# Loads of bias rows, steps of modulation and the order of two mixers' side work in a two-block transformer kernel

## The chip, the cores and the metric

One core of one Trainium2 chip runs the whole program. Its engines are TensorE (PE, with its weight loads as PEld), VectorE (DVE), ScalarE (ACT), GpSimd (POOL, unused here) and SyncE (SP), which issues nearly all DMA transfers from one in-order queue. The metric is the device time of one execution in microseconds (us), the median of several.

## The reference

The input is x of 256 tokens by 1024. The first block adds a hybrid mixer (dilated attention and a state space scan) and a SwiGLU; the second adds two layers. Each of those is modulated by a condition vector, and the second of them has the mixer that most of the change is about. Cut to what matters:

```python
mx = jnp.split((c_act @ w_mod[l] + b_mod[l])[:, None, :], N_MOD, axis=-1)   # modulation, 2 layers
x = x + 0.5 * mx[2] * swiglu_2(modulate(rms_norm(x), mx[0], mx[1]), *ffn1)
h = modulate(rms_norm(x), mx[3], mx[4])
# layer 0: mix_window_diff (heads of h @ ab_w_in); layer 1, the last mixer:
cq, dq, ckv, dk, dv = split_cols(h @ w_in, CD_SPLITS)              # 768, 512, 288, 512, 512
ckv_c, dk_c, dv_c = split_cols(hc @ w_in[:, CD_Q_WIDTH:], CD_SPLITS[2:])
q = mla_queries(cq, c_q_a_norm, c_w_uq, ...)                       # low rank norm, then up
kn, kr, v = mla_keys_values(ckv, c_kv_a_norm, c_w_ukv, ...)
y_mla = sweep_blocks(lambda q_blk, n: mla_attend(q_blk, kn_all, kr_all, v_all), q, Q_BLOCK)
y_nat = neighbourhood_attention(dq, dk, dv, dk_c, dv_c, d_rpb)     # with a relative bias per grid offset
y = jnp.concatenate([y_mla, y_nat], axis=-1) @ w_out
x = x + mx[5] * y
x = x + 0.5 * mx[8] * swiglu_2(modulate(rms_norm(x), mx[6], mx[7]), *ffn2)
```

## The kernel before, in words

Every matrix is cut into chunks of 128 by up to 1024 numbers (up to 512 KB). A chunk goes through a ring of six slots: SP loads it (`load_chunk`, L283) once the chunk six places before it has been used, ACT rounds it to a high part (`split_hi`, L289), DVE takes the low part (`split_lo`, L295), and PE multiplies high by high, high by low and low by high (`product`, L347). ACT and DVE split three chunks ahead of PE (`LEAD`). Results lie in three PSUM banks; a bank is free again when ACT has copied it out (L422 for `LinearT`) or DVE has (L442, L449).

The program is a list of stages, each with steps. A step has a part for SP, PE, ACT and DVE, and every engine runs its parts in the order of one common list. So a wait in one step holds all that stands behind it on that engine, and SP's transfers of later steps are issued only after those of earlier steps. `woven` mixes tracks of stages by their share of the segment; `beside(base, side, per)` (L1315) puts side steps after the base step that their number names, at most `per` of them after each.

Three places matter here.

**Modulation** (L668). Per layer, 9 rounds of 8 chunks of `w_mod` (512 KB each) are multiplied with the two condition vectors: 8 matmuls of the profile a chunk, on four 32 column tiles of the array (`chunk`, L725). They have a ring of six slots of their own. A step is two chunks; a further step of each round turns the row of results (L712). Layer 0's stage is woven along the first block's projections, layer 1's from 0.1 to 0.95 of the segment that ends the first block, and that begins with the last chunks of `w_attn_branch`, the eight of `w_out`, and the norm before the feed-forward. SP loads six chunks at the stage's first step, and then the chunk that is six places on whenever one is used.

**Head work.** `HeadNorms` normalises the heads of a projection (squares on ACT L1358, sums on DVE L1371, the scale L1362 and L1363 on ACT, the products L1381 to L1398 on DVE; item j is applied in step j + 2). `Turns` transposes them on PE (L1450) through one bank, which ACT empties (L1460) before the next turn may begin. Both are side steps, of projections and of attention.

**The last mixer.** Its 44 weight chunks are those of cq (6), ckr for x and for the context (4 and 4), dk (4 and 4), dq (4), dv (4 and 4), w_uq (6) and w_ukv (2 and 2). `GridLoad` is one stage ahead of them: when all of the modulated norm is there, SP issues 32 transfers of 64 KB each, in pieces of 64 numbers, that lay out the bias rows of neighbourhood attention (`grid_rows`). Then `Attend` works on pairs of heads, 8 pairs of the neighbourhood and 8 of the low rank attention: scores L1519 (and the bias by L1525), maxima on DVE (L1604 or L1615), exponentials on ACT (L1561), transposes L1536, values L1548, each pair spread over four steps. `mla_heads` (the norms of the low rank queries and keys, steps `m_steps`), `SpreadKeys` and the turns of their results stand beside these pairs.

```python
        alone(norm, grid_load, Merged(beside(steps_of(*cd_main[1:], u_q, u_kv_x, u_kv_c), side, per=2)))
        side = [(0, (spread, 0)), (0, m_steps[4]), (0, m_steps[5])]
        side += [(1, m_steps[6]), (1, m_steps[7]), (1, t_steps[14]), (1, t_steps[15])]
        side += [(2, m_steps[8]), (2, m_steps[9]), (2, t_steps[16]), (2, t_steps[17])]
        side += [(3 + n // 2, t_steps[18 + n]) for n in range(8)]
```

## Time and profile before

| | us |
|---|---|
| median of 3 runs (2728.10 to 2730.65) | 2728.46 |
| the profiled execution | 2728.05 |
| its span in the trace | 2726.2 |
| PE busy (15262 matmuls) | 2538.7, 93% of the span |
| PE weight loads busy | 2152.0, 79% |
| DVE busy | 1350.0, 50% |
| ACT busy | 1018.4, 37% |
| moved by DMA | 372.23 MB, 137 GB/s in the mean |

The span is the time from the first to the last instruction of the trace; 1.85 us of the execution lie around it. The chain of waits, followed back from the end, is 85% PE. The granted clock has two levels, 2.4 GHz (1.00 in the rows) and 1.2 GHz (0.50); its mean is 0.965. So the time is that of PE's work and of the places at which PE stands still or goes slowly, and these are what is looked for.

### The profile page before, as it was taken

How to read it: one execution, taken by the hardware profiler on the slowest of the kernel's cores; microseconds unless marked ns; L12 is line 12 of the kernel's file. 1: busy time of each engine (PE TensorE's matmuls, PEld its weight loads, DVE VectorE, ACT ScalarE, POOL GpSimd, SP SyncE). 2: the span in 40 equal slices, each digit the busy share in tenths (PEclk: the TensorE clock that was granted, in tenths of full speed). 3: DMA queues.
4: the chain of work that ended last, by engine and by line, in shares of the span. 5: the costliest groups of instructions: out<-in, count | busy, mean ns of one | idle time of the engine just before them, and what ended most of it. 6: DMA issues, size and time to landing. Idle time of an engine off the chain costs nothing.

```text
span 2726.2 us, 36254 instructions
## 1 busy us (share of the span) xinstructions
PE 2538.7 (93%) x15262; PEld 2152.0 (79%) x15262; DVE 1350.0 (50%) x2221; ACT 1018.4 (37%) x1633; POOL 0.2 (0%) x4
## 2 busy tenths in 40 slices
PE   7999999899989999989778999998999986978998
PEld 6888789888867888868566888886888866758998
DVE  4646464654454333357866333334333344656654
ACT  4534444433343222145542222223222224643542
POOL 0000000000000000000000000000000000000000
PEclk8999999999989999989889999999999997989999
DMA  8886743488843333335002333332333325502554
GB/s 280 281 270 194 227 128 101 156 312 305 312 143 93 93 101 93 101 109 185 16 1 77 94 100 93 101 93 77 96 98 98 95 76 146 166 7 63 164 185 132
DMA packets 145476, 372.23 MB, mean 137 GB/s; under 512 B 20234, under 2 KB 65570, under 8 KB 145186
## 3 DMA queue, kind: packets, MB, share of 16 engines
q1 hardware_dynamic: 144882, 368.21, 42.9%
q8 instruction: 122, 2.00, 0.3%
q10 hardware_dynamic: 432, 1.69, 0.2%
q14 instruction: 40, 0.33, 0.0%
HBM read 368.71 MB, written 1.15 MB: 136 GB/s over the span
## 4 chain that ended last, share of the span: by engine, by line
PE 85%; DVE 7%; ACT 4%; issue 1%; SPq 1%; DMA 1%; ACTq 0%; DVEq 0%
PE psum L347 74%; PE psum L725 2%; PE psum L1548 1%; PE psum L1519 1%; DVE normed_raw L533 1%; DVE normed_lo L546 1%; PE psum L1536 1%; SPq L1798 1%; PE psum L1450 1%; PE psum L1138 1%; PE psum L939 1%; ACT weights_hi L289 1%; PE psum L494 1%; PE psum L1150 1%; ACT arena L1561 1%
## 5 line engine op out<-in xcount | busy, mean ns | idle before, releaser
L295 DVE TENSOR_TENSOR weights_lo<-weights_raw,weights_hi 128x1024 fp32r<-128x1024 f32 (+3 forms) x547 | 657.6, 1213 | 528.5 <-ACT weights_hi L289 525.9
L347 PE MATMUL psum<-normed_hi,weights_hi 128*128 128x256 f32 (+1 forms) x2560 | 864.4, 338 | 34.7 <-DVE normed_lo L546 23.8
L347 PE MATMUL psum<-normed_lo,weights_hi 128*128 128x256 f32 (+1 forms) x2560 | 848.5, 331 | 0.0
L347 PE MATMUL psum<-normed_hi,weights_lo 128*128 128x256 f32 (+1 forms) x2560 | 847.6, 331 | 0.0
L289 ACT CAST weights_hi<-weights_raw 128x1024 fp32r<-128x1024 f32 (+3 forms) x547 | 563.0, 1035 | 394.8 <-DMA weights_raw<-in_w_down 266.9
L347 PEld LDWEIGHTS psum<-normed_hi,weights_hi 128*128 128x128 f32 x2560 | 489.4, 191 | 119.9 <-issue 53.1
L347 PEld LDWEIGHTS psum<-normed_hi,weights_lo 128*128 128x128 f32 x2560 | 490.3, 192 | 44.8
L347 PEld LDWEIGHTS psum<-normed_lo,weights_hi 128*128 128x128 f32 x2560 | 490.7, 192 | 43.9 <-issue 1.2
L347 PE MATMUL psum<-hidden_hi,weights_hi 128*128 128x512 f32 x528 | 205.4, 389 | 0.0
L347 PE MATMUL psum<-hidden_lo,weights_hi 128*128 128x512 f32 x528 | 205.4, 389 | 0.0
L347 PE MATMUL psum<-hidden_hi,weights_lo 128*128 128x512 f32 x528 | 205.4, 389 | 0.0
L347 PE MATMUL psum<-weights_hi,normed_hi 128*128 128x512 f32 (+3 forms) x368 | 144.5, 393 | 40.3 <-ACT arena L422 20.9
L449 DVE SCALAR_TENSOR_TENSOR resid<-psum,mod,resid 128x256 f32<-128x256 f32 x80 | 35.8, 480 | 275.4 <-PE psum L347 275.4
L585 DVE TENSOR_TENSOR arena<-arena,psum 128x512 f32<-128x512 f32 (+1 forms) x110 | 64.0, 581 | 205.4 <-PE psum L347 205.4
L577 ACT CAST hidden_hi<-arena 128x512 fp32r<-128x512 f32 x66 | 41.0, 621 | 309.3 <-DVE arena L585 309.3
L574 ACT ACTIVATE arena<-psum 128x512 f32<-128x512 f32 (+1 forms) x110 | 56.4, 513 | 247.7 <-PE psum L347 247.6
L347 PE MATMUL psum<-weights_hi,normed_lo 128*128 128x512 f32 (+3 forms) x368 | 140.6, 382 | 0.0
L347 PE MATMUL psum<-weights_lo,normed_hi 128*128 128x512 f32 (+3 forms) x368 | 139.8, 380 | 0.0
L347 PEld LDWEIGHTS psum<-weights_hi,normed_hi 128*128 128x128 f32 x368 | 75.6, 205 | 57.1 <-ACT arena L422 21.1
L347 PEld LDWEIGHTS psum<-hidden_hi,weights_lo 128*128 128x128 f32 x528 | 99.1, 188 | 20.7
L347 PEld LDWEIGHTS psum<-hidden_lo,weights_hi 128*128 128x128 f32 x528 | 99.1, 188 | 20.6
L347 PEld LDWEIGHTS psum<-hidden_hi,weights_hi 128*128 128x128 f32 x528 | 99.1, 188 | 20.4
(254 smaller groups left out, 2794.1 us busy)
## 6 DMA issues: line engine op xcount, KB each, us to landing
weights_raw<-in_w_gu SPq DMA_DIRECT2D x220, 512.0 KB, 3.5
weights_raw<-in_w_down SPq DMA_DIRECT2D x110, 512.0 KB, 3.5
arena<-in_w_mod SPq DMA_DIRECT2D x72, 512.0 KB, 6.3
weights_raw<-in_w_x SPq DMA_DIRECT2D x24, 512.0 KB, 4.7
resid<-in_w_mod SPq DMA_DIRECT2D x24, 512.0 KB, 6.1
normed_raw<-in_w_mod SPq DMA_DIRECT2D x24, 512.0 KB, 5.8
under_normed_hi<-in_w_mod SPq DMA_DIRECT2D x24, 512.0 KB, 6.4
weights_raw<-in_w_qk SPq DMA_DIRECT2D x24, 512.0 KB, 4.0
```

Of the source, the lines that this page charges most:

```text
L289: se.copy(w_hi[:, c % RING, a], w_raw[:, c % RING, a]).then_inc(hi_ready, 1)
L295: ve.tensor_tensor(w_lo[:, c % RING, a], w_raw[:, c % RING, a], w_hi[:, c % RING, a].bitcast(F32), ALU.subtract).then_inc(lo_ready, 1)
L347: last = te.matmul(out, a, b, start=start and n == 0, stop=stop and n == 2)
L449: last = ve.scalar_tensor_tensor(out=resid[:, k, mine], in0=psum[:, self.bank(k), side * S - at0:(side + 1) * S - at0], scalar=mod[:, m, s ...
L494: last = te.matmul(psum[:, NORM_BANK, 0:w], ones, self.squares_at[:, k, :], start=(k == 0), stop=(k == KD - 1))
L533: last = ve.scalar_tensor_tensor(out=dest[:, k, a], in0=resid[:, k, a], scalar=self.gain(k, side), in1=rstd[:, a], op0=ALU.mult, op1=ALU.mult)
L546: last = ve.scalar_tensor_tensor(out=lo[:, a], in0=raw[:, a], scalar=self.shift(k - 1, side), in1=hi[:, a].bitcast(F32), op0=ALU.add, op1= ...
L574: se.activation(raw, self.sums(b), ACT.Silu).then_inc(evac_act, 1)
L577: se.copy(hi, raw).then_inc(hid_hi, 1)
L585: ve.tensor_tensor(raw, raw, self.sums(b), ALU.mult).then_inc(evac_dve, 1)
L725: last = te.matmul(psum[32 * g:32 * g + 32, MOD_BANK, 0:MOD_W], cond[:, k, :], self.ring[c % MOD_RING][:, g, :], start=k == 0, stop=k == K ...
L939: last = te.matmul(psum[:, SIDE + i % 2, j * S:(j + 1) * S], ident[0:SH, h:h + 1].to_broadcast([SH, P]), la_t, start=True, stop=True)
```

## The change

Four things are done. Modulation takes four chunks to a step, so that a round has two such steps and one that turns. The grid loads become a stage of eight steps of four transfers, one after every second weight chunk of the last mixer from its first chunk on. In the last mixer dq comes before dk, dv of the context comes last, behind w_uq and w_ukv, and the head work is set anew: the first eight steps of `mla_heads`, `SpreadKeys` and two turns stand beside projections, and attention begins with what is left. In the layer before, the last four head norms and four turns beside attention come three steps later, and two side steps may follow one step.

```diff
@@ class Modulation
-                self.n = MOD_ROUNDS * (KD // 2 + 1) + 1
+                self.n = MOD_ROUNDS * (KD // 4 + 1) + 1
...
-                r, k = divmod(i, KD // 2 + 1)
-                return self.first + r, 2 * k - 2
+                r, k = divmod(i, KD // 4 + 1)
+                return self.first + r, 4 * k - 4
...
-                    for m in range(2):
+                    for m in range(4):
                         self.load(sp, (r - self.first) * KD + k + m + MOD_RING)
...
-                    self.chunk(pe, r, k)
-                    self.chunk(pe, r, k + 1)
+                    for m in range(4):
+                        self.chunk(pe, r, k + m)
@@ class GridLoad
+            n = NT * 4
...
-                sp.wait_ge(*self.after)
-                for t in range(NT):
-                    for rl in range(2):
-                        for h in range(8):
+                if i == 0:
+                    sp.wait_ge(*self.after)
+                t, pair = divmod(i, 4)
+                for rl in range(2):
+                    for h in (2 * pair, 2 * pair + 1):
@@ attention of layer 0
-        side = [(0, s) for s in h_steps[14:18]] + [(4, s) for s in t_steps[10:14]]
+        side = [(3 + n, step) for n, step in enumerate(h_steps[14:18])]
+        side += [(7 + n // 2, step) for n, step in enumerate(t_steps[10:14])]
...
-        alone(Merged(beside(steps_of(attend), side)))
+        alone(Merged(beside(steps_of(attend), side, per=2)))
@@ the last mixer
-                (x_t, "w_ckr", KVR + ROPE, ckr), (ctx_t, "w_ckr", KVR + ROPE, ckr),
-                (x_t, "w_dk", WT, dk), (ctx_t, "w_dk", WT, dk), (x_t, "w_dq", WT, dq),
-                (x_t, "w_dv", WT, dv), (ctx_t, "w_dv", WT, dv))])
+                (x_t, "w_ckr", KVR + ROPE, ckr), (ctx_t, "w_ckr", KVR + ROPE, ckr), (x_t, "w_dq", WT, dq),
+                (x_t, "w_dk", WT, dk), (ctx_t, "w_dk", WT, dk), (x_t, "w_dv", WT, dv))])
...
+        cd_main += [u_q, u_kv_x, u_kv_c, LinearT(W["w_dv"], KD, WT, normed, ctx_t, dv)]
...
-        side += [(28, t_steps[n]) for n in range(8, 12)] + [(30, t_steps[12]), (30, t_steps[13])]
+        side += [(22, h_steps[12]), (22, h_steps[13]), (24, t_steps[8]), (24, t_steps[9])]
+        side += [(26, h_steps[14]), (26, h_steps[15]), (27, h_steps[16]), (27, h_steps[17])]
+        side += [(28 + n, t_steps[10 + n]) for n in range(4)]
         m_steps = steps_of(mla_heads)
-        side += [(40, m_steps[n]) for n in range(4)]
-        alone(norm, grid_load, Merged(beside(steps_of(*cd_main[1:], u_q, u_kv_x, u_kv_c), side, per=2)))
+        side += [(36 + n, m_steps[n]) for n in range(4)] + [(40, m_steps[4]), (40, m_steps[5])]
+        side += [(41, (spread, 0)), (41, m_steps[6]), (42, t_steps[14]), (42, t_steps[15]), (42, m_steps[7])]
+        base_steps = beside(steps_of(*cd_main[1:]), [(2 * n, step) for n, step in enumerate(steps_of(grid_load))])
+        places = [n for n, (stage, _) in enumerate(base_steps) if stage is not grid_load]
+        side = [(places[j], step) for j, step in side]
+        alone(norm, Merged(beside(base_steps, side, per=2)))
         segments[-1] = (segments[-1][0], 0)
-        side = [(0, (spread, 0)), (0, m_steps[4]), (0, m_steps[5])]
-        side += [(1, m_steps[6]), (1, m_steps[7]), (1, t_steps[14]), (1, t_steps[15])]
-        side += [(2, m_steps[8]), (2, m_steps[9]), (2, t_steps[16]), (2, t_steps[17])]
-        side += [(3 + n // 2, t_steps[18 + n]) for n in range(8)]
+        side = [(0, m_steps[8]), (0, m_steps[9]), (0, t_steps[16]), (1, t_steps[17])]
+        side += [(1 + n // 2, t_steps[18 + n]) for n in range(8)]
```

Left out are the renumbering of the head items and turns that follows from dq standing before dk, and the copy of a modulation round, which now waits in the step that begins at chunk 4 of it.

The SP queue at the start of the last mixer (weights_raw<-in_w_... is a weight chunk, arena<-scratch_rpb a grid transfer), as a difference:

```order
 L283 DMA weights_raw<-in_w_cq 128x1024 x6
-L1798 DMA arena<-scratch_rpb 64x4x64 x32
-L283 DMA weights_raw<-in_w_ckr 128x576 x8
-L283 DMA weights_raw<-in_w_dk 128x1024 x8
...
+L283 DMA weights_raw<-in_w_ckr 128x576
+L1800 DMA arena<-scratch_rpb 64x4x64 x4
+L283 DMA weights_raw<-in_w_ckr 128x576 x2
+L1800 DMA arena<-scratch_rpb 64x4x64 x4
+L283 DMA weights_raw<-in_w_ckr 128x576 x2
```

The 32 transfers stood in one piece ahead of the seventh chunk; now the seventh chunk goes first, and four transfers stand between every two chunks.

PE at the end of `w_out` in the first block, before (merged is the input of `w_out`, L725 modulation, L490 the sum of the norm, normed the input of the feed-forward):

```order
L347 MATMUL psum<-merged_hi,weights_lo 128x256
L725 MATMUL psum<-arena,cond 32x256 x8
L347 MATMUL psum<-merged_hi,weights_hi 128x256
...
L725 MATMUL psum<-arena,cond 32x256 x8
L490 MATMUL psum<-squares,const 128x256
L725 MATMUL psum<-arena,cond 32x256 x8
L347 MATMUL psum<-normed_hi,weights_hi 128x256
```

and in the changed kernel:

```order
L347 MATMUL psum<-merged_hi,weights_lo 128x256
L725 MATMUL psum<-arena,cond 32x256 x16
L490 MATMUL psum<-squares,const 128x256
L347 MATMUL psum<-normed_hi,weights_hi 128x256
```

Before, the first step of modulation cut `w_out` two chunks from its end, a second stood before the sum of the norm and a third behind it. Now one step of four chunks stands after the last chunk of `w_out`.

PE at the start of attention in the last mixer, before (L1519 and L1525 are a pair's scores, L1450 x8 two turns, L1536 and L1548 transposes and values):

```order
L1519 MATMUL psum<-arena 128x512 x2
L1525 MATMUL psum<-arena,const 128x256 x2
L1519 MATMUL psum<-arena 128x512 x2
L1525 MATMUL psum<-arena,const 128x256 x2
L1450 MATMUL psum<-const,arena 96x128 x8
L1519 MATMUL psum<-arena 128x512 x2
L1525 MATMUL psum<-arena,const 128x256 x2
L1536 MATMUL psum<-const,arena 128x128 x8
L1450 MATMUL psum<-const,arena 96x128 x8
```

and in the changed kernel:

```order
L1519 MATMUL psum<-arena 128x512 x2
L1525 MATMUL psum<-arena,const 128x256 x2
L1450 MATMUL psum<-const,arena 96x128 x4
L1519 MATMUL psum<-arena 128x512 x2
L1525 MATMUL psum<-arena,const 128x256 x2
L1450 MATMUL psum<-const,arena 96x128 x12
L1519 MATMUL psum<-arena 128x512 x2
L1525 MATMUL psum<-arena,const 128x256 x2
L1536 MATMUL psum<-const,arena 128x128 x8
L1450 MATMUL psum<-const,arena 96x128 x8
```

The twelve turns beside attention have become ten: two (L1450 96x128 x8) now stand before the last chunk of dv. The others begin one step sooner and are done at the fifth pair, where before they were done at the seventh.

## Rows read from the trace of the kernel before

**Rows 1.** The waits of PE, whole run (us in total, times, longest us).
```profile
PE psum L347 <- ACT arena L422: 24.2, 4, 20.9
```

**Rows 2.** Timeline of the SP queue (start us, us, what, count).
```profile
2238.22 21.05 SPq L1798 DMA_DIRECT2D arena<-scratch_rpb  x32
```

**Rows 3.** Timeline of ACT in the same stretch (in brackets: idle before, and what ended it).
```profile
2263.71 0.67 ACT L289 CAST weights_hi<-weights_raw 128x576 fp32r<-128x576 f32 x1 [23.60 <-DMA weights_raw<-in_w_ckr]
...
2271.81 0.66 ACT L422 ACTIVATE arena<-psum 128x256 f32<-128x256 f32 x2 [5.31 <-PE psum L347]
```

**Rows 4.** Timeline of TensorE's weight loads in the same stretch.
```profile
2239.53 0.19 PEld L347 LDWEIGHTS psum<-weights_hi,normed_hi 128*128 128x128 f32 x1 [1.39 <-DVE weights_lo L295]
...
2264.93 0.29 PEld L347 LDWEIGHTS psum<-weights_hi,normed_hi 128*128 128x128 f32 x1 [21.14 <-ACT arena L422]
```

**Rows 5.** Busy time in stretches (busy us by engine, clock, DMA share, GB/s).
```profile
50.00:100.00 50.00, 50.00 (x462) 45.12 (x463) 38.97 (x63) 28.05 (x48) 0.00 (x0) 1.00 0.90 287
...
2245.00:2252.00 7.00, 0.00 (x0) 0.00 (x0) 0.00 (x0) 0.00 (x0) 0.00 (x0) 0.59 0.55 101
```

**Rows 6.** Timeline of PE at the start of attention in the last mixer.
```profile
2385.26 1.13 PE L1519 MATMUL psum<-arena 64*128 64x512 f32 x4 [1.17 <-ACT arena L422]
...
2394.29 1.09 PE L1450 MATMUL psum<-const,arena 128*96 128x128 f32 x4 [4.72 <-DVE arena L1398]
...
2401.35 2.08 PE L1519 MATMUL psum<-arena 64*128 64x512 f32 x4
...
2418.12 0.61 PE L1450 MATMUL psum<-const,arena 128*96 128x128 f32 x4 [0.97 <-ACT under_normed_hi L1460]
2418.66 1.13 PE L1519 MATMUL psum<-arena 64*128 64x512 f32 x4
...
2443.97 0.60 PE L1519 MATMUL psum<-under_normed_hi,normed_raw 96*128 96x256 f32 x2
```

**Rows 7.** Timeline of DVE at a maximum there.
```profile
2441.12 0.69 DVE L1615 CUSTOM_DVE_ANT_0 arena<-psum,const 128x512 f32<-128x512 f32 x1 [3.66 <-PE psum L1525]
```

**Rows 8.** Timeline of ACT at an exponential there.
```profile
2442.47 0.72 ACT L1561 ACTIVATE arena<-arena,small 128x512 f32<-128x512 f32 x1 [2.87 <-DVE small L1615]
```

**Rows 9.** The page's costliest groups: count, then busy us and mean ns.
```profile
L295 DVE TENSOR_TENSOR weights_lo<-weights_raw,weights_hi 128x1024 fp32r<-128x1024 f32 (+3 forms) x547 | 657.6, 1213 | 528.5 <-ACT weights_hi L289 525.9
```

**Rows 10.** Timeline of PE around one step of modulation.
```profile
59.73 0.28 PE L347 MATMUL psum<-normed_hi,weights_lo 128*128 128x256 f32 x1
...
60.94 0.39 PE L347 MATMUL psum<-normed_hi,weights_hi 128*128 128x256 f32 x1
```

**Rows 11.** Timeline of PE at the first steps of modulation.
```profile
18.56 0.64 PE L725 MATMUL psum<-resid,cond 128*32 128x256 f32 x8 [2.48 <-DMA resid<-in_w_mod]
...
34.54 1.94 PE L725 MATMUL psum<-normed_raw,cond 128*32 128x256 f32 x16
```

**Rows 12.** Timeline of DVE at the end of w_out in the first block.
```profile
536.37 0.42 DVE L442 TENSOR_TENSOR resid<-resid,psum 128x256 f32<-128x256 f32 x1 [0.28 <-PE psum L347]
...
539.24 0.42 DVE L442 TENSOR_TENSOR resid<-resid,psum 128x256 f32<-128x256 f32 x1 [0.28 <-PE psum L347]
```

**Rows 13.** Timeline of PE in the same place.
```profile
542.46 0.64 PE L725 MATMUL psum<-arena,cond 128*32 128x256 f32 x8 [3.26 <-DMA arena<-in_w_mod]
543.71 1.08 PE L725 MATMUL psum<-arena,cond 128*32 128x256 f32 x8 [0.61 <-DMA arena<-in_w_mod]
...
552.90 1.07 PE L725 MATMUL psum<-arena,cond 128*32 128x256 f32 x16
554.40 0.70 PE L490 MATMUL psum<-squares,const 128*128 128x256 f32 x2 [0.43 <-DVE squares L460]
...
558.02 0.36 PE L347 MATMUL psum<-normed_hi,weights_hi 128*128 128x256 f32 x1 [1.92 <-DVE normed_lo L541]
```

**Rows 14.** Timeline of DVE at the start of attention in the first mixer of the second block.
```profile
1303.10 1.23 DVE L1604 TENSOR_REDUCE small<-psum 128x2 f32<-128x1024 f32 x1 [1.46 <-PE psum L1519]
...
1309.20 0.75 DVE L1627 SCALAR_TENSOR_TENSOR arena<-arena,small 128x512 f32<-128x512 f32 x1
```

More of the change, by code:

```diff
@@ L731, in scalar @@
                 r, k = self.at(i)
-                if k == KD - 2:
+                if k == KD - 4:
                     act.wait_ge(mod_used, KD * (r + 1))
@@ L1991, in build @@
         u_kv_c = LinearT(W["w_ukv"], KVR // P, WT, ckv_t, ctx_t, kv)
+        cd_main += [u_q, u_kv_x, u_kv_c, LinearT(W["w_dv"], KD, WT, normed, ctx_t, dv)]
+        cd_main[-1].ready = norm.ready
         def whole(a, t, start, width):
@@ L2021, in build @@
                                 [part[:, m, :] for part in ckv_t], col("ckv_norm", m), pair=True) for m in range(KVR // P)]
-        turn_items += [TurnItem([dk[:, t, m * P:(m + 1) * P] for t in range(TT)], [heads.done(13)], dk_t[:, m, :])
+        turn_items += [TurnItem([dq[:, t, (m + j) * P:(m + j + 1) * P] for j in range(2) for t in x_t], [heads.done(11)],
+                                dq_t[:, m:m + 2, :], HD ** -0.5) for m in (0, 2)]
+        turn_items += [TurnItem([dk[:, t, m * P:(m + 1) * P] for t in range(TT)], [heads.done(15)], dk_t[:, m, :])
                        for m in range(4)]
-        turn_items += [TurnItem([dq[:, t, (m + j) * P:(m + j + 1) * P] for j in range(2) for t in x_t], [heads.done(15)],
-                                dq_t[:, m:m + 2, :], HD ** -0.5) for m in (0, 2)]
         turn_items += [TurnItem([mq[:, t, (h + j) * MQ:(h + j + 1) * MQ] for j in range(2) for t in x_t], [mla_heads.done(3)],
```

13 lines of the change are left out of this document (6 added, 7 removed).

## The prediction

> **What bounds the kernel now.** I read the waits of PE first, since the chain of waits runs 85% over PE. Most of them are short and spread out; one is not: a single wait of 20.9 us for ACT's copy of a PSUM bank, L422 [rows 1]. The queue of SP shows what is behind it: 32 grid transfers are issued from 2238.22 for 21.05 us, 0.66 us each, and only then the next weight chunk [rows 2]. ACT splits three chunks ahead, so it stands for 23.60 us until that chunk lands, with the copy of the bank behind it in its order [rows 3]; PE starts the chunk at 2239.53, uses what it has, and then waits 21.14 us to load a weight [rows 4]. The stretch inside has a granted clock of 0.59 and DMA engines 55% busy [rows 5], so after the stall PE also goes at the lower of its two levels.
>
> The second place is the start of attention behind it: from the first pair's scores at 2385.26 to the ninth's at 2443.97 take 58.7 us, with waits of PE for turns that wait for head norms [rows 6]. The third is spread over the whole first block: each step of modulation holds PE, and one of them stops it in the middle of `w_out` [rows 10 to 13].
>
> **The grid loads.** 32 issues of 0.66 us stay. They now stand in groups of four, 2.63 us, between pairs of weight chunks. The seventh chunk is issued ahead of them, when chunk 1 is used. The first group waits for the norm as before and is issued from 2238.2 to 2240.9; the eighth and ninth chunk follow at once, before PE needs them. PE starts the fourth chunk at 2239.53 [rows 4]; three chunks at 2.87 us (the distance of two copies [rows 12]) bring it to 2248.1, where the seventh begins. Before, it began when the sixth was copied, 2271.8 [rows 3]. That is **-23.7 us**, slow clock included. The cover of the rest: from here the ckr chunks are small, 0.56 of a full one by their 576 columns, so two of them take PE some 3.2 us, and SP needs 2.63 and two weight issues for them, 3.3 us. SP falls behind by little in three such rounds, and has six slots of lead; then come full chunks, 5.7 us a pair. If that lead were gone, ACT would wait again, some 1 us a round. I add 1 us for it below.
>
> By the Trainium skill, page DMA: Bandwidth & Descriptors, section Issuing engines are not separate DMA queues, the time to initiate a DMA is "usually small relative to the DMA itself". Here the trace differs: the transfers keep the engines 55% busy while SP is busy all the time, so issue is the longer of the two. By the rule the packets would be what holds the weights, and parting the issues would leave most of the stall; that is the first rival.
>
> **Attention of the last mixer.** Before, the first two pairs have 2 head steps and the spreading of keys, then 2 and two turns, then 2 and two turns beside them; the third pair comes 16.1 us after the first and the fifth 33.4 us after it [rows 6]. Now the last two head steps and one turn stand after the first pair, three turns after the second, then two each. I follow it: an operation of DVE over 128x512 is 0.69 us and a maximum is two of them [rows 7], as is the product of one head norm, of which two stand before the second maximum; an exponential is 1.52 [rows 8], a turn 0.6 [rows 6] with as much for its copy. That puts the third pair at 12.7 us after the first, the fourth at 21.4, the fifth at 28.4, the sixth at 35, and the three after it, with no double turn, 4.7 apart: the ninth at 49.5. Before it was 58.7 [rows 6]. **-9 us**. These steps have gone beside the context's dv, four chunks or 11.5 us of PE. DVE has for them four splits of 1.2 us [rows 9] and head work of some 16 operations, 10.9 us, 15.8 in all, so it ends about 1.5 us late for the first maximum, and the first of the two turns waits up to 2. In return the turns of dk stand one to a step: a second turn in a step waits 0.97 us for the first one's copy [rows 6], and three of these go. With the 1 us of SP from above: **+1.5 us**, between -4 (no backlog at all) and +6 (DVE's whole excess over PE's 11.5 us, and the 2 us of the turn).
>
> **Modulation.** A step of two chunks costs PE 1.21 us from the last matmul before to the first after it, less the usual 0.12 (2.87 for 24 [rows 12]): 1.09 [rows 10]. A lone chunk of 8 matmuls takes 0.64, two take 1.07 [rows 13], so a chunk is 0.43 and the change to and from this kind of matmul 0.23; the first matmul after it is longer by 0.11 (0.39 for 0.28 [rows 10]). That makes 0.34 a step. There are 36 steps of chunks a layer, now 18.
>
> Layer 0: 18 fewer steps. One of them was free, since the first stood in PE's wait for the first norm [rows 11]; now the first stands behind the small dt product, where two chunks take 1.94 at the slow clock [rows 11], and I count 1.7 for two more. 17 x 0.34 - 1.7 = **-4.1 us**. PE is busy without a break where I looked (50.00 of 50 us [rows 5]), so this arrives.
>
> Layer 1: the first step waited 3.26 and 0.61 us for its chunks in the middle of `w_out`, and the two last chunks of `w_out` came out at 552.90, partly at the slow clock [rows 13]. Now these run on: 539.24 plus 2 x 2.87 [rows 12] is 545.0. The chunks of modulation landed at 542.46 and 543.71 [rows 13], 1.25 apart, so the fourth at 546.2; the step ends at 546.7. The sum of the norm came 1.5 us behind `w_out`, it is at 547.1 now; from there to the feed-forward 3.6 us as before (554.40 to 558.02 [rows 13]): 550.7 for 558.0, -7.3. By 558.0 six chunks had been done, now four: +0.9. Behind it 33 steps become 17: 16 x 0.34 = 5.4. Together **-11.8 us**. If the fourth chunk lands a burst later, by up to 4 us, that comes off.
>
> By the Trainium skill, page TensorE: Matmul & The Clock Gate, section Part 3: Packing small matmuls, a pack of column tiles takes one matmul's time and some 4 ns a tile; no price for entering or leaving is stated. The trace has 0.34 us a step; by the page the halving of the steps would bring nothing. That is the second rival.
>
> **Attention of layer 0.** The first pair's maximum starts at 1303.10 and its last product at 1309.20 [rows 14]; one head step stands between them, and three more in the next pairs. Without them at most 1309.20 - 1303.10 - 1.2 = 4.9 us can be won, less what comes back: the same four norms later, where DVE also has pairs with a bias, and two steps with two turns, 1 us each by the second turn's wait [rows 6]. Between -4.9 and +2; DVE has slack later, but only part: **-1.5 us**.
>
> **Sum**, against the profiled execution's 2728.05 (0.4 below the median, whose runs lie within 2.6): -23.7 - 9 + 1.5 - 4.1 - 11.8 - 1.5 = -48.6, so 2679.5; I say **2680**. A measurement of this kernel tells 0.2%, 5.5 us, from no change.
>
> **Rivals.**
> - *Packets hold the weights, not issue.* The engines were busy 55% of the 21.05 us [rows 5]: 11.6 us. If this time stays, since every weight chunk lies behind 1024 small pieces, the time is 2680 + 11.6 = 2691.5. For it: pieces of 64 numbers. Against: they are spread over 16 engines and over some 28 us now. Chance 0.12.
> - *A step's price does not halve.* If the 0.34 us belongs to chunks and not to steps, 33 x 0.34 = 11.2 us fall away: 2691. Against: the lone chunk's 0.64 [rows 13]. 0.07.
> - *The backlog of DVE eats the gain of attention.* If head steps beside the context's dv make DVE late by their whole 5 us and the second pair waits for it and the turns too, the 9 us are gone: 2689. 0.12.
> - *More than counted*: layer 0's attention brings its 4.9 and the projections wait less, 2670. 0.04.
> - *Slower: bursts of modulation starve the weights.* In the first block the DMA engines are busy 0.90 at 287 GB/s [rows 5]. A step now asks for four chunks at once, 2.1 MB or 7.3 us at that rate, and a weight chunk asked for behind them lands that much later. Its slack is three chunks of 2.87, 8.6 us, until ACT splits it, and three more until PE. It decides if a step's four loads and the weights between cannot be moved in the time of that step; then PE waits at each of 35 steps. 1.5 us at each undoes the forecast, 2 us gives 2680 + 70 = 2750. Against: the rate needed rises by 2% only (0.34 in 15 us), and the rows show 10% free. 0.03.
>
> **How the numbers follow.** The forecast has 0.62, with its own range 2672 to 2688. The rivals on the slower side of it lie at 2689 to 2692. The range is 2668 to 2693: it takes in all but the last rival and the far ends. Of the last rival's 0.03 a third falls within 0.2%. Faster by over 0.2% 0.97, within 0.01, slower 0.02.
>
> **What would show it.** SP's queue must have eight groups of 2.6 us with weight issues between, and no wait of PE for L422 over 2 us there. The seventh chunk should begin about 2248 less what was gained before (some 17 us), so at 2231. A step of modulation must take 2.07 us from the last matmul before it to the first after it (4 x 0.43 + 0.23 + 0.12). `w_out` must end without a DMA wait inside. The ninth pair must come about 50 us after the first. It is wrong if ACT waits for weights in the last mixer by more than 5 us in all, if DMA waits appear before L725 or L347 in the first block, or if the first pair's scores of the last mixer do not come some 40 us earlier than before.

## The result, and the profile after

The changed kernel takes **2699.49 us** (median of 4, 2697.82 to 2701.74) beside 2728.28 for the kernel before on the same chip: a ratio of 0.9894, interval 0.9877 to 0.9911, or 29 us. The forecast was 2680, the range 2668 to 2693. The direction was right and the size a good half of what was forecast. The profiled execution took 2701.74 us, with a span of 2700.0 (2726.2 before), PE busy 2537.1 us (2538.7) and a mean granted clock of 0.966 (0.965).

**The stall at the grid loads is gone.** The waits of PE of the changed kernel, the line that answers to [rows 1], whose longest was 20.9 us (the 2.8 of it lie in the first block, the rest in the last mixer):

```profile
PE psum L347 <- ACT arena L422: 4.0, 2, 2.8
```

The SP queue of the changed kernel, in place of the one row of 21.05 us in [rows 2]:

```profile
2234.13 0.33 SPq L283 DMA_DIRECT2D weights_raw<-in_w_ckr  x1
2239.94 2.61 SPq L1800 DMA_DIRECT2D arena<-scratch_rpb  x4
2242.60 1.08 SPq L283 DMA_DIRECT2D weights_raw<-in_w_ckr  x2
2243.72 2.56 SPq L1800 DMA_DIRECT2D arena<-scratch_rpb  x4
2246.32 1.18 SPq L283 DMA_DIRECT2D weights_raw<-in_w_ckr  x2
```

These are the first two of eight groups, of 2.6 to 3.2 us, with weights between them; the seventh chunk is issued at 2234.13, ahead of all. PE begins it at 2249.85 (2271.61 before), where the prediction had 2231: the stall is gone, but what was to be gained ahead of it is not there.

**Modulation.** PE around a step of four chunks, which answers to [rows 10]:

```profile
66.29 0.28 PE L347 MATMUL psum<-normed_hi,weights_lo 128*128 128x256 f32 x1
66.50 1.07 PE L725 MATMUL psum<-normed_raw,cond 128*32 128x256 f32 x16
67.39 1.05 PE L725 MATMUL psum<-under_normed_hi,cond 128*32 128x256 f32 x16
68.37 0.39 PE L347 MATMUL psum<-normed_hi,weights_hi 128*128 128x256 f32 x1
```

From 66.29 to 68.37 are 2.08 us; 2.07 was forecast. And the end of `w_out`, as in [rows 13]:

```profile
545.13 1.50 PE L725 MATMUL psum<-arena,cond 128*32 128x256 f32 x24
546.89 0.64 PE L725 MATMUL psum<-arena,cond 128*32 128x256 f32 x8 [0.25 <-DMA arena<-in_w_mod]
547.46 0.70 PE L490 MATMUL psum<-squares,const 128*128 128x256 f32 x2
551.08 0.55 PE L347 MATMUL psum<-normed_hi,weights_hi 128*128 128x256 f32 x1 [2.92 <-DVE normed_lo L541]
```

Forecast were the step at 545.0, the feed-forward at 550.7. It begins at 551.08, where before it began at 558.02.

**The last mixer.** PE at the start of its attention, for [rows 6] (L1519 begins a pair; L1450 is a turn):

```profile
2368.93 1.13 PE L1519 MATMUL psum<-arena 64*128 64x512 f32 x4 [1.17 <-ACT arena L422]
...
2379.22 0.84 PE L1450 MATMUL psum<-const,arena 128*96 128x128 f32 x4 [3.61 <-ACT normed_raw L1460]
2380.84 1.06 PE L1450 MATMUL psum<-const,arena 128*96 128x128 f32 x4 [0.77 <-ACT under_normed_hi L1460]
2381.83 2.08 PE L1519 MATMUL psum<-arena 64*128 64x512 f32 x4
...
2405.48 1.13 PE L1519 MATMUL psum<-arena 64*128 64x512 f32 x4
...
2420.01 0.60 PE L1519 MATMUL psum<-under_normed_hi,normed_raw 96*128 96x256 f32 x2
```

The ninth pair comes 51.1 us after the first (49.5 forecast, 58.7 before), the third after 12.9 (12.7), the sixth after 36.6 (35). But the first pair itself is only 16.3 us earlier than before, where the forecast said some 40. The loss must lie ahead of it.

**Where it lies.** I took the same matmul of PE in both timelines at the borders of the terms. The changed kernel is ahead by 1.1 us at 387, 12.2 at 824, 11.1 at the first pair of attention of layer 0 (1301.93 before). Behind that attention (1442.76 before) it is **1.6 us late**. It is 1.9 late at 2215 and 21.3 ahead at 2269, behind the old stall; 16.3 at the first pair of the last mixer, 24.0 at the ninth. The last 2.3 us of the span's 26.2 come after PE's last matmul. So a term forecast at -1.5 came out at +12.7. Here is PE in that attention, in the pairs beside which the head norms and turns stand now:

```profile
1305.36 1.13 PE L1519 MATMUL psum<-arena 64*128 64x512 f32 x4
1309.30 0.63 PE L1536 MATMUL psum<-const,arena 128*128 128x128 f32 x4 [2.82 <-DVE arena L1627]
...
1310.75 1.13 PE L1519 MATMUL psum<-arena 64*128 64x512 f32 x4
1314.62 1.94 PE L1536 MATMUL psum<-const,arena 128*128 128x128 f32 x8 [2.74 <-ACT arena L1561]
...
1323.89 0.63 PE L1450 MATMUL psum<-const,arena 128*128 128x128 f32 x4 [1.47 <-ACT arena L1460]
1324.45 1.83 PE L1519 MATMUL psum<-arena 64*128 64x512 f32 x4
```

PE stands 2.8 us for DVE (and for the exponential behind it) in one pair after another, then the eight matmuls of L1536 take 1.94 us and the four of L1519 1.83, where they take 1.1 and 1.13 elsewhere, and a second turn in the same step waits 1.47 us for the first one's copy. Such waits stand in the kernel before too, though (3.02 us at 1310.01, 2.13 at 1315.27), so they can't be read as the loss. What the loss consists of shows in the busy time of the whole stretch, from the first pair to the same matmul behind the attention (us of the stretch, then busy us of PE, PEld, DVE, ACT and POOL, the granted clock, DMA share, GB/s). Before, in the changed kernel, and in two kernels of the experiments below, e1 and e6:

```profile
1301.93:1442.76 140.83, 111.92 (x677) 82.76 (x677) 103.22 (x306) 69.22 (x197) 0.00 (x0) 0.89 0.03 8
1290.87:1444.38 153.51, 123.46 (x677) 91.88 (x677) 103.49 (x306) 69.93 (x197) 0.00 (x0) 0.83 0.02 8
1291.76:1433.58 141.82, 113.60 (x677) 83.37 (x678) 103.23 (x306) 69.20 (x197) 0.00 (x0) 0.88 0.03 8
1290.72:1437.42 146.70, 114.03 (x677) 84.07 (x677) 103.38 (x306) 69.58 (x197) 0.00 (x0) 0.88 0.03 8
```

The same 677 matmuls take 11.5 us longer in the changed kernel, at a granted clock of 0.83 for 0.89. The time in which PE does nothing grows by 1.1 us only, from 28.9 to 30.1. So nearly the whole loss is matmuls at the lower clock, and not waiting.

### The profile page after: what moved, and what is told of

Same layout as the page of the kernel before. It is cut to its first block, busy times and chain, and to the rows that moved or that the text cites. A ratio compares the mean times of both kernels' runs of the same rounds, so it can differ in the third digit from the quotient of the medians.

```text
span 2700.0 us, 36253 instructions
## 1 busy us (share of the span) xinstructions
PE 2537.1 (94%) x15262; PEld 2163.9 (80%) x15262; DVE 1350.3 (50%) x2221; ACT 1021.5 (38%) x1633; POOL 0.2 (0%) x4
## 4 chain that ended last, share of the span: by engine, by line
PE 87%; DVE 7%; ACT 4%; issue 1%; DMA 1%; SPq 0%; ACTq 0%; DVEq 0%
PE psum L347 74%; PE psum L725 2%; PE psum L1548 2%; PE psum L1519 1%; DVE normed_raw L533 1%; PE psum L1536 1%; DVE normed_lo L546 1%; PE psum L1450 1%; DVE weights_lo L295 1%; PE psum L1138 1%; PE psum L939 1%; ACT arena L1561 1%; PE psum L1150 1%; DVE arena L1615 1%; ACT weights_hi L289 1%
## 5 line engine op out<-in xcount | busy, mean ns | idle before, releaser
L347 PE MATMUL psum<-normed_hi,weights_hi 128*128 128x256 f32 (+1 forms) x2560 | 863.2, 337 | 36.8 <-DVE normed_lo L546 24.8
L347 PE MATMUL psum<-normed_lo,weights_hi 128*128 128x256 f32 (+1 forms) x2560 | 849.2, 332 | 0.0
L347 PE MATMUL psum<-normed_hi,weights_lo 128*128 128x256 f32 (+1 forms) x2560 | 848.9, 332 | 0.0
L347 PEld LDWEIGHTS psum<-normed_hi,weights_hi 128*128 128x128 f32 x2560 | 490.8, 192 | 112.2 <-issue 47.2
L347 PEld LDWEIGHTS psum<-normed_lo,weights_hi 128*128 128x128 f32 x2560 | 492.1, 192 | 44.0 <-issue 1.2
L347 PEld LDWEIGHTS psum<-normed_hi,weights_lo 128*128 128x128 f32 x2560 | 491.6, 192 | 44.3
L347 PE MATMUL psum<-hidden_hi,weights_hi 128*128 128x512 f32 x528 | 205.4, 389 | 0.0
L347 PE MATMUL psum<-hidden_lo,weights_hi 128*128 128x512 f32 x528 | 205.4, 389 | 0.0
L347 PE MATMUL psum<-hidden_hi,weights_lo 128*128 128x512 f32 x528 | 205.4, 389 | 0.0
L449 DVE SCALAR_TENSOR_TENSOR resid<-psum,mod,resid 128x256 f32<-128x256 f32 x80 | 35.8, 480 | 273.6 <-PE psum L347 273.6
L347 PE MATMUL psum<-weights_hi,normed_hi 128*128 128x512 f32 (+3 forms) x368 | 144.5, 393 | 26.5 <-DVE weights_lo L295 15.3
L347 PE MATMUL psum<-weights_hi,normed_lo 128*128 128x512 f32 (+3 forms) x368 | 139.2, 378 | 0.0
L347 PE MATMUL psum<-weights_lo,normed_hi 128*128 128x512 f32 (+3 forms) x368 | 138.8, 377 | 0.0
L347 PEld LDWEIGHTS psum<-hidden_hi,weights_lo 128*128 128x128 f32 x528 | 99.1, 188 | 20.6
L347 PEld LDWEIGHTS psum<-hidden_hi,weights_hi 128*128 128x128 f32 x528 | 99.1, 188 | 20.6
L347 PEld LDWEIGHTS psum<-hidden_lo,weights_hi 128*128 128x128 f32 x528 | 99.1, 188 | 20.5
L347 PEld LDWEIGHTS psum<-weights_hi,normed_hi 128*128 128x128 f32 x368 | 74.8, 203 | 42.6 <-issue 21.2
```

Source lines behind the costliest of these rows:

```text
L347: last = te.matmul(out, a, b, start=start and n == 0, stop=stop and n == 2)
L449: last = ve.scalar_tensor_tensor(out=resid[:, k, mine], in0=psum[:, self.bank(k), side * S - at0:(side + 1) * S - at0], scalar=mod[:, m, s ...
```

## The experiments

All times are medians, the ratios against the kernel before on the same chip. Every kernel computes the whole reference. The table is the sum of the prediction as measured: what each profiled kernel gains (-) or loses (+) against the profiled kernel before in each stretch, from the starts of the same matmuls of PE (e11 stands apart, below).

| us | median | mod. layer 0, 24 to 387 | mod. layer 1, to 824 | attention layer 0, 1302 to 1443 | grid, 2215 to 2269 | to 1st pair, 2385 | to 9th pair, 2444 |
|---|---|---|---|---|---|---|---|
| forecast | 2680 | -4.1 | -11.8 | -1.5 | -23.7 | +1.5 | -9 |
| the change | 2699.5 | -1.3 | -11.1 | +12.7 | -23.2 | +5.0 | -7.6 |
| e1 | 2689.3 | -1.1 | -11.1 | +1.0 | -23.1 | +4.8 | -9.5 |
| e2 | 2736.0 | -0.3 | -2.0 | +11.4 | -0.8 | -0.8 | -0.1 |
| e3 | 2719.2 | -3.9 | -11.1 | +6.1 | +0.6 | -1.5 | +1.2 |
| e4 | 2708.4 | -0.5 | -2.0 | +7.2 | -22.8 | +2.2 | 0.0 |
| e5 | 2701.8 | -3.7 | -10.8 | +12.2 | -22.6 | +5.5 | -7.5 |
| e6 | 2693.8 | -3.7 | -10.6 | +5.9 | -23.2 | +6.6 | -9.6 |
| e7 | 2726.0 | +0.1 | -1.9 | +4.6 | -0.5 | +4.4 | -9.6 |
| e8 | 2692.9 | -1.1 | -11.2 | +2.6 | -23.2 | +5.1 | -7.7 |
| e9 | 2687.9 | -1.1 | -11.1 | +1.0 | -23.0 | +2.6 | -9.4 |
| e10 | 2693.5 | -3.7 | -10.7 | +1.0 | -23.0 | +5.0 | -9.6 |
| e12 | 2686.2 | -1.3 | -11.3 | +1.1 | -23.0 | +2.4 | -10.7 |

**e1_old_attention0**: the changed kernel with one part undone.

```diff
-        side = [(3 + n, step) for n, step in enumerate(h_steps[14:18])]
-        side += [(7 + n // 2, step) for n, step in enumerate(t_steps[10:14])]
+        side = [(0, s) for s in h_steps[14:18]] + [(4, s) for s in t_steps[10:14]]
...
-        alone(Merged(beside(steps_of(attend), side, per=2)))
+        alone(Merged(beside(steps_of(attend), side)))
```

> The changed kernel with the side steps beside attention of layer 0 as they were before (head norms after steps 0 to 3, turns from step 4 on, one side step after each). Theory A: the new places of these steps cost what the two traces differ by across this attention, from 11.1 us ahead before it to 2.6 us behind after it, 13.7 us. Then this kernel takes 2699.5 - 13.7 = 2686 us (2683 to 2689), and PE is 9 to 12 us ahead of the kernel before at the end of that attention. Rival B: the loss comes with the earlier start of this attention (another phase of TensorE's granted clock), whatever stands beside it. Then this kernel takes 2697 to 2702 us.

2689.26 us (2689.03 to 2690.39), ratio 0.9856 (0.9839 to 0.9872). The attention is back at +1.0. Theory A holds, 0.3 us above its range: 10.2 us in the medians, 11.7 in the traces, and the executions of the two kernels don't meet (2689.0 to 2690.4 and 2697.8 to 2701.7). Of the 11.7 us, 9.9 are PE's busy time (123.46 for 113.60).

**e2_only_attention0**: the same two places, changed on the kernel before.

> The kernel before with the new places of the side steps beside attention of layer 0 and nothing else. Theory A: 2728.3 + 13.7 = 2742 us (2739 to 2745), with waits of PE for DVE at pairs 4 to 6, the lower clock behind them and turns in pairs that PE waits for. Rival B (the loss belongs to the start of attention being earlier): 2726 to 2731 us.

2735.95 us, ratio 1.0024 (1.0013 to 1.0035). Slower, so B falls, but by 7 us and not by 14, although its trace shows +11.4 in the attention. What is wrong is the yardstick: the next two kernels keep the old order there and lose 6 to 7 us against the profiled kernel before all the same. In them PE is busy 119.4 and 123.4 us in this stretch, at a clock of 0.84 and 0.80, where the profiled kernel before has 111.9 at 0.89.

**e3_only_modulation**: the kernel before with the part `class Modulation` of the change.

> The kernel before with only modulation at four chunks to a step. Theory A: by the two traces the changed kernel is 12.2 us ahead once modulation is done, and none of the rest depends on it: 2728.3 - 12.2 = 2716 us (2714 to 2719). Rival B: the earlier start of what follows moves the clock's phase in attention and takes it back: 2726 to 2731 us. In layer 0 I expect the same give-back as in the changed kernel: about 5.5 us ahead at 315 us, 1 to 2 us ahead at 400 us.

2719.21 us, ratio 0.9965 (0.995 to 0.9981): 9.6 us for the 12.2 of A, just above its range. Layer 0 gives 3.9 here and keeps it, against what I expected.

**e4_only_grid_spread**: the kernel before with the grid in eight steps.

```diff
-        alone(norm, grid_load, Merged(beside(steps_of(*cd_main[1:], u_q, u_kv_x, u_kv_c), side, per=2)))
+        base_steps = beside(steps_of(*cd_main[1:], u_q, u_kv_x, u_kv_c),
+                            [(2 * n, step) for n, step in enumerate(steps_of(grid_load))])
+        places = [n for n, (stage, _) in enumerate(base_steps) if stage is not grid_load]
+        side = [(places[j], step) for j, step in side]
+        alone(norm, Merged(beside(base_steps, side, per=2)))
```

> The kernel before with the grid transfers in eight steps of four, one after every second weight chunk of the last mixer, and the old order of its projections and side steps. Theory C: the stall goes (22.9 us in the changed kernel up to the ckr chunks) and nothing of it is given back: 2728.3 - 23 = 2705 us (2703 to 2708), with 58 to 59 us from the first to the ninth pair of its attention. Rival D: the 4.6 us that the changed kernel lost in the projections behind that point come from SP's queue, where the spread transfers stand, not from the new order; then this kernel loses them too and takes 2710 us (2708 to 2713).

2708.39 us, ratio 0.9922 (0.9904 to 0.9941). The time is on the border of C and D; the trace has 22.8 gained and 2.2 given back before the first pair. With the new order alone (e7) 4.4 are given back, with both (e1) 4.8. So most of the 5.0 us belongs to the order, and D holds for at most the smaller half.

**e5_turns_single** and **e6_heads_early** take the change in attention of layer 0 apart (each a diff on the changed kernel):

```diff
# e5
-        side += [(7 + n // 2, step) for n, step in enumerate(t_steps[10:14])]
+        side += [(7 + n, step) for n, step in enumerate(t_steps[10:14])]
-        alone(Merged(beside(steps_of(attend), side, per=2)))
+        alone(Merged(beside(steps_of(attend), side)))
# e6
-        side = [(3 + n, step) for n, step in enumerate(h_steps[14:18])]
+        side = [(n, step) for n, step in enumerate(h_steps[14:18])]
```

> The changed kernel, but beside attention of layer 0 only one side step may follow a step, so that the four turns stand one to a step (7 to 10) and not in two pairs (7 and 8). The head norms keep their new places (3 to 6). The stretch from the first to the thirteenth pair is 53.6 us in the changed kernel and 47.6 before; the pairs with the head norms take 5.4 and 7.3 us there (4.5 and 3.3 before) and the two with paired turns 7.3 and 3.8 behind a 6.4. If the turns in pairs are what costs, this kernel gains 4 us or more: 2693 to 2696 us. If the head norms in the pairs with a bias are (PE stands 2.8 us for DVE in each, and the lower clock follows), it stays at 2698 to 2701 us.

> The changed kernel with the last four head norms of layer 0 beside steps 0 to 3 as before, and the four turns at their new, paired places (steps 7 and 8). If the head norms cost: back to e1_old_attention0 but for two second turns of 1 us, 2689.3 + 2 = 2691 us (2689 to 2693). If the turns cost: 2696 to 2700 us.

e5: 2701.79 us (0.9896, 0.9881 to 0.991), 1 us above the second expectation. e6: 2693.79 us (0.9863, 0.9847 to 0.988), 1 us above the range of what was expected. Moving the head norms back gains 5.7 us. The turns at their new places cost as well: e6 stays 4.5 us above e1 (2 by the ratios, 4.9 in the traces), where 2 were expected. The two costs are of different kinds. In e6 PE's busy time is that of e1 (114.0 for 113.6 us), and it stands still 32.7 us for 28.2: the turns cost waiting. From e6 to the changed kernel the busy time grows by 9.4 us and the standing still falls by 2.6: the later head norms cost clock. The us from one pair to the next (starts of L1519):

```
pair to pair   1-2  ...                                       12-13
change         1.8 3.0 2.8 3.7 3.2 5.4 7.3 6.4 7.3 3.8 4.9 4.0   13-20: 4.9 2.8 6.7 3.8 3.7 3.4 4.1   23-28: 4.6 3.8 3.8 3.8 4.2
e1             1.8 3.0 5.2 6.9 4.5 3.2 3.9 4.3 3.8 3.8 5.2 2.9   13-20: 4.9 2.8 5.1 3.8 3.7 3.4 4.1   23-28: 3.7 2.1 2.5 2.1 4.6
e5             1.8 3.0 2.6 3.9 3.0 5.4 7.2 4.4 4.3 4.3 3.8 2.5   13-20: 3.4 7.3 4.0 5.2 7.0 6.4 5.9   23-28: 4.1 3.2 2.1 2.2 4.9
e4             0.9 3.0 5.2 6.9 4.3 3.5 3.6 4.3 3.8 3.8 5.3 2.9   13-20: 4.9 2.8 5.6 4.9 3.6 3.4 4.1   23-28: 3.9 3.8 3.8 3.8 4.2
```

From the first to the thirteenth pair e5 takes 2.6 us less than e1 (46.2 for 48.8). From the fourteenth to the twentieth it takes 12.9 more (35.8 for 22.9), though no head norm or turn of the moved ones stands there. But e5 does more than part the turns: with one side step to a step, the two steps that normalise the first output tile (L1728, L1742) and its turns, which stand at steps 8, 9, 10 and 12 in e1, are pushed to steps 11 to 14. DVE begins the first of them at 1338.80, ahead of the fourteenth pair's maximum, and in that pair PE waits 3.19 us for DVE. From the fourteenth to the seventeenth pair e5 loses 4.8 us (16.5 for 11.7), and from there to the twentieth 8.0 (19.3 for 11.2), at the lower clock. So e5 doesn't say what paired turns alone cost. Busy time in stretches of e5 (PE, PEld, DVE, ACT, POOL, then clock, DMA share, GB/s):

```profile
1336.00:1344.00 8.00, 4.13 (x25) 2.26 (x23) 6.63 (x23) 4.44 (x12) 0.00 (x0) 1.00 0.00 0
...
1360.00:1368.00 8.00, 8.00 (x38) 7.23 (x37) 4.93 (x16) 2.88 (x9) 0.00 (x0) 0.50 0.01 2
1368.00:1376.00 8.00, 8.00 (x37) 6.90 (x38) 3.38 (x11) 1.61 (x7) 0.00 (x0) 0.50 0.00 0
```

the same of the changed kernel, at pairs 22 to 27:

```profile
1376.00:1384.00 8.00, 4.16 (x29) 3.07 (x28) 6.44 (x30) 5.23 (x19) 0.00 (x0) 0.92 0.00 0
1384.00:1392.00 8.00, 8.00 (x36) 6.36 (x35) 3.85 (x14) 2.97 (x13) 0.00 (x0) 0.50 0.01 2
1392.00:1400.00 8.00, 8.00 (x36) 6.46 (x36) 6.66 (x24) 3.43 (x15) 0.00 (x0) 0.50 0.00 0
```

and of e1, at the pairs of the one (16 to 20) and of the other (24 to 27):

```profile
1352.00:1360.00 8.00, 7.71 (x63) 6.39 (x61) 5.18 (x14) 4.60 (x15) 0.00 (x0) 1.00 0.01 2
1360.00:1368.00 8.00, 7.31 (x61) 6.29 (x60) 6.63 (x24) 3.13 (x12) 0.00 (x0) 1.00 0.01 2
...
1376.00:1384.00 8.00, 5.80 (x45) 4.54 (x45) 5.79 (x26) 5.68 (x21) 0.00 (x0) 1.00 0.01 2
```

At the full clock PE has room in these pairs, little in the one (busy 7.31 to 7.71 of 8 us) and more in the other (5.80). At the lower level it has none, busy 8.00 of 8.00, and a pair of 2.1 to 3.8 us takes 3.8 to 7.0. So the clock decides what the attention costs, and each stretch of 16 us at the lower level is worth 5 us or more. In the changed kernel 5.8 of the 12.7 us are lost up to the thirteenth pair and 5.3 from the 22nd to the 28th, beside which nothing was moved; e4, with the old places, has the same slow stretch there.

**e7_only_last_mixer_order**: the change's last part on the kernel before, with `alone(norm, grid_load, Merged(beside(steps_of(*cd_main[1:]), side, per=2)))`.

> The kernel before with only the new order of the last mixer's projections, head norms and turns; the grid transfers stand in one piece as before. By e1_old_attention0 against e4_only_grid_spread the order brings 27.7 - 20.8 = 6.9 us across the last mixer: 9.5 in the attention, less some 3 that PE waits for DVE beside the last chunks of dv. If it does so without the spread as well: 2729 - 7 = 2722 us (2719 to 2725). If its gain needs the spread (or hides in the clock): within 3 us of before.

2725.99 us, ratio 0.9988 (0.9979 to 0.9997): 3 to 4 us, below the 7 expected and between the two expectations. In the trace 4.4 us are lost ahead of the first pair and 9.6 won up to the ninth, net 5.2. The order works without the spread, for less.

**e8_heads_alternate**, an attempt at something better, on the changed kernel. Left out of the diff are the turns of each tile's output, two steps later (`8 * t + 12` and `8 * t + 14`), and the sorting of the side steps:

```diff
-        side = [(3 + n, step) for n, step in enumerate(h_steps[14:18])]
-        side += [(7 + n // 2, step) for n, step in enumerate(t_steps[10:14])]
+        side = [(2 * n + 1, step) for n, step in enumerate(h_steps[14:18])]
+        side += [(8 + n, step) for n, step in enumerate(t_steps[10:14])]
...
```

> The changed kernel with the four head norms of layer 0 beside steps 1, 3, 5 and 7, the turns one to a step at 8 to 11, and the turns of each tile's output two steps later. If only DVE's total work bounds the first 13 pairs, its place doesn't matter so long as no pair is left waiting behind two head norms in a row: 2686 to 2691 us, as e1_old_attention0 or a little below. If any head norm beside a pair with a bias costs 2 us or more, 2692 to 2697 us.

2692.86 us (0.9862, 0.9848 to 0.9877): 3.6 above e1, in the second expectation. In the trace only 1.6 of it are lost in this attention; another 1.8 are lost in the last mixer's, which e8 doesn't touch. No gain.

**e9_two_steps_back**, on e1, for the term that came out at +5.0. Busy time in stretches of the changed kernel there: DVE at 4.76 to 4.90 of 5 us, PE down to 2.53:

```profile
2350.00:2355.00 5.00, 5.00 (x23) 4.14 (x23) 4.86 (x10) 4.50 (x11) 0.00 (x0) 1.00 0.58 203
2355.00:2360.00 5.00, 4.06 (x18) 3.01 (x17) 4.76 (x17) 2.02 (x5) 0.00 (x0) 1.00 0.59 198
2360.00:2365.00 5.00, 2.53 (x11) 2.08 (x12) 4.90 (x12) 3.27 (x7) 0.00 (x0) 0.74 0.37 107
2365.00:2370.00 5.00, 3.83 (x16) 2.17 (x14) 4.25 (x6) 2.65 (x6) 0.00 (x0) 0.92 0.22 53
```

```diff
-        side += [(41, (spread, 0)), (41, m_steps[6]), (42, t_steps[14]), (42, t_steps[15]), (42, m_steps[7])]
+        side += [(41, (spread, 0)), (42, t_steps[14]), (42, t_steps[15])]
...
-        side = [(0, m_steps[8]), (0, m_steps[9]), (0, t_steps[16]), (1, t_steps[17])]
-        side += [(1 + n // 2, t_steps[18 + n]) for n in range(8)]
+        side = [(0, m_steps[6]), (0, m_steps[7]), (0, t_steps[16]), (1, m_steps[8]), (1, m_steps[9]), (1, t_steps[17])]
+        side += [(2 + n // 2, t_steps[18 + n]) for n in range(8)]
```

> The kernel of e1_old_attention0 with two of the eight low rank head steps (the seventh and eighth) moved from beside the context's dv back to the first pair of attention, the ninth and tenth to the second pair, and the turns behind them one pair later. Theory A: DVE is what is late beside dv (busy 4.8 to 4.9 of every 5 us from 2350 to 2370 in the changed kernel), and a head step moved from there takes its 2.4 us of DVE with it. PE then waits 3 to 4 us less before the first pair and the second to fourth pair come 4 to 5 us later after it: 2689 to 2693 us. Rival: the wait beside dv is for something else (ACT, or transfers behind the grid); then nothing is gained there and attention still loses: 2693 to 2696 us.

2687.87 us (0.9852, 0.9838 to 0.9867), below both expectations; the 1.4 us to e1 are within what executions differ by, so what follows is read from the traces. The first pair is 2.2 us less late (+2.6 for +4.8) and the ninth keeps its distance (49.3 us for 49.2); 1.3 of it is lost again behind the ninth. DVE's backlog is a cause, as in A, of 2.2 of the 4.8 us at least; that attention would pay 4 to 5 us for it was wrong.

**e10_grid_eights**, on e1: `n = NT * 2` steps, `for h in range(4 * half, 4 * half + 4)`, and places `4 * n` for `2 * n`.

> The kernel of e1_old_attention0 with the grid transfers in four groups of eight (5.3 us of SP each), one after every fourth weight chunk. If the issue time of SP is the cost and its six slots of lead the cover, a group of 5.3 us between four small chunks (6.4 us of PE) still fits, and the time is within 2 us of 2689.3. If the lead is gone by the second group, ACT waits for a chunk behind each of the first two groups, 2 to 3 us each: 2692 to 2695 us.

Its four executions took 2688.28, 2689.53, 2697.47 and 2697.59 us, at mean granted clocks of 0.970, 0.970, 0.966 and 0.966. The profiled one (2689.53) has the same +5.0 as e1: eight to a group fit as well, as first expected. The median of 2693.5 says nothing of it.

**e11_modulation_eights**, on e1: `KD // 8`, `8 * k - 8`, `range(8)` and `KD - 8` in `Modulation`.

> The kernel of e1_old_attention0 with modulation eight chunks to a step, a whole round, in the same ring of six. By the price of a change of matmul kind, 0.34 us, it would gain 18 x 0.34 = 6 us: 2683 us. But the last two chunks of a step are asked for only when its first two are used; they take some 6 us to land, and PE is there after 2.6 us. A wait of 4 to 5 us in each of 18 steps, partly at the lower clock: 2689 + 75 = 2765 us (2740 to 2800).

2808.87 us (two executions), ratio 1.0294 (1.0272 to 1.0317): 120 us above e1 and not 75, outside the range. A step takes 7.3 to 14.8 us. PE in one of them:

```profile
81.42 1.05 PE L725 MATMUL psum<-resid,cond 128*32 128x256 f32 x16
86.01 0.64 PE L725 MATMUL psum<-normed_raw,cond 128*32 128x256 f32 x8 [3.54 <-DMA normed_raw<-in_w_mod]
87.56 1.08 PE L725 MATMUL psum<-normed_raw,cond 128*32 128x256 f32 x8 [0.91 <-DMA normed_raw<-in_w_mod]
88.57 0.58 PE L347 MATMUL psum<-normed_hi,weights_hi 128*128 128x256 f32 x1
```

Both waits stand before the last two chunks, as expected, and the matmuls of L347 behind them take 0.41 us for 0.28, the lower clock. The ring of six covers a step of four chunks, and not one of eight.

**e12_single_turns**, on e9:

```diff
-        side += [(2 + n // 2, t_steps[18 + n]) for n in range(8)]
+        side += [(j, t_steps[18 + n]) for n, j in enumerate((2, 2, 3, 3, 4, 5, 6, 7))]
```

> The kernel of e9_two_steps_back with the last four of the eight key turns of the last mixer one to a step (steps 4 to 7) and not in pairs (steps 4 and 5). There the two pairs with a double turn take 6.7 us and the two without any 4.7, 22.8 in all. If the double turn costs by PE's wait for the first one's copy (0.97 us), as in the sum, four steps with one turn each take 5.2 to 5.4: 2687.9 - 1.5 = 2686.4 us (2684.5 to 2688.5). If a turn costs the same alone, no difference: 2687 to 2689 us.

2686.19 us (2684.31 to 2687.18), ratio 0.9852 (0.9833 to 0.987), 13 us below the changed kernel and the lowest median of all. Three of the four pairs with one turn take 5.2 us:

```profile
2380.47 1.13 PE L1519 MATMUL psum<-arena 64*128 64x512 f32 x4
2385.63 1.13 PE L1519 MATMUL psum<-arena 64*128 64x512 f32 x4
2390.79 1.13 PE L1519 MATMUL psum<-arena 64*128 64x512 f32 x4
2395.96 1.13 PE L1519 MATMUL psum<-arena 64*128 64x512 f32 x4
```

The fourth takes 6.7, since another turn (`t_steps[26]`) already stood at step 7, and the second of the two waits 0.96 us: 22.2 us in all for 23.3 in e9. The medians don't show the gain. The distance to e9, 1.7 us, is as forecast, but the kernel before took 3.5 us less on this chip too (2726.5 for 2730.0), and the ratios of e9 and e12 are the same.

## Why the prediction was right, and where it failed

- **Grid loads, -23.7: right.** -23.2, and -22.6 to -23.2 in every kernel that spreads them. The first rival (packets hold the weights) would have left 11.6 of it. SP's share of what came back is 2.2 us at most (e4), for the 1 that was set.
- **Modulation, the step: right.** 0.34 us a step, to the hundredth; the second rival falls. **Layer 1, -11.8:** -11.1, but 1.9 to 2.0 of it is no effect: e2, e4 and e7 leave modulation alone and have it too, so the profiled kernel before was unlucky there. **Layer 0, -4.1:** -3.7 to -3.9 in four kernels and -1.1 to -1.3 in five with the same steps, the changed kernel among them. The difference is clock again: in the changed kernel 24 matmuls behind a wait at 355.75 take 4.43 us for 3.11 in e3, and the sixteen of L1013 that begin at 303.73 and 316.75 take 3.41 and 2.78 us for 2.89 and 1.99, together 2.6 us.
- **Attention of layer 0, -1.5 between -4.9 and +2: the step that failed.** It came out at +12.7, 14.2 of the 22.4 us by which the spans' difference (26.2) fell short of the sum (48.6). Part of that is the yardstick: of the profiled kernels with the old places the one before is the fastest here. By medians the new places cost 10.2 us on the changed kernel (e1) and 7 on the kernel before (e2). The prediction priced the four head steps by DVE's time, which the first pairs do win: the sixth comes 14.5 us after the first, in e1 21.6. It priced what comes back by waits, DVE's slack in the later pairs and 1 us for each second turn, and gave every matmul its full clock. PE's standing still hardly changed (28.9 us before, 30.1 now). The term that it put at nothing was the clock: the same 677 matmuls took 123.5 us for 111.9. Its upper end of +2 came from a row for two turns in a step, in which the clock was full. No row of attention at the lower level was in the sum, though the trace of before has some: at 2401.35 L1519 takes 2.08 us for 1.13 [rows 6]. That the new places lower the clock rests on the changed kernel and e5 (eight executions at 0.964 to 0.967) beside e1, e9 and e12 (twelve at 0.969 to 0.971). The places aren't all of it, since two of e10's four executions, with the old places, stand at 0.966 as well, and how they do it stays open.
- **Projections, +1.5 between -4 and +6:** +5.0, by the mechanism named as the third rival (DVE's backlog beside the context's dv, e9), inside its bounds and mis-sized. "DVE ends about 1.5 us late" was the number, from 15.8 us of DVE's work beside dv; DVE is busy 18.8 of the 20 us from 2350 to 2370, with its first wait (0.72 us) before 2369.43. e9 moves two of the steps away and gets 2.2 us back; what makes the rest I did not part.
- **Attention of the last mixer, -9:** -7.6, and -9.4 to -9.6 in e1, e6, e7, e9 and e10. In the changed kernel L1519 takes 2.08 us at the third pair, a stretch at the lower clock. The following was close (third pair 12.9 for 12.7, ninth 51.1 for 49.5), though its own steps give 49.1 for the ninth: 35 and three times 4.7.
- **Slower: modulation starves the weights.** Not at four chunks: from 20 to 830 us PE waits 0.3 us in all for a DMA, 4.7 before. At eight something else did it, the ring.

Without the failed part (e1) the change takes 2689.3 us, inside the range, still 9 above the forecast.

## What to carry to other kernels

Where an attention or any stretch alternates between engines, compare PE's busy time for the same matmuls before blaming its waits, and price a moved step twice: at TensorE's full clock and at half, with what a unit of the loop takes at either (here 3.4 to 3.7 us in e1 and 6.4 to 7.0 in e5 for the same pair). A range that takes its upper end from rows at the full clock is too narrow. And before an expected gain of under 10 us is read from two profiles, look at the same stretch in a kernel that doesn't touch it: here it differed by up to 7 us.

## What the runs showed that I had not expected

- **One program, 9 us apart, and the clock with it.** e10's four executions stand in two pairs, 2688 and 2697 us, with the mean granted clock at 0.970 and 0.966. The kernel before took from 2720.61 us (0.967) to 2734.92 (0.961) in all these comparisons. e1 stayed within 1.4 us at 0.969.
- **The clock can stay low under a busy PE.** In e5 and in the changed kernel PE is busy 8.00 of 8.00 us in two stretches on end at a granted clock of 0.50. The matmuls there are small transposes and values, of 128 and 64 columns. The Trainium skill, page TensorE: Matmul & The Clock Gate, section Part 1: The HAM clock gate, has the full clock come back once the array has been busy. That doesn't show in these two stretches, as far as the busy time of instructions tells. The same section of the Trainium skill puts the penalty of the ramp, the matmuls until the clock has risen, under 1% of a typical kernel's span. The 5 to 13 us by which stretches of these kernels differ are under 0.5% of 2700, but the clock falls again and again here: by a mean of 0.966 over the changed kernel some 6.8% of its span lie at the lower level (an estimate, twice what is missing to 1.00). What makes the clock fall in one kernel and not in another is not settled: in e2 and in the changed kernel a stretch with PE busy 4.2 of 8 us came right before it, in e5 one of 5.4 (with one of 4.1 two stretches earlier), in e4 one of 6.2.
- **An attention in which nothing was changed varies too.** With the same side steps at the same places PE was busy 111.9 us in attention of layer 0 before, 113.6 in e1, e9, e10 and e12, and 119.2 to 123.4 in e3, e4 and e7.
